# Prompt attention on one Trainium2 core: two heads side by side in four strips, scores ahead of transposes, and the selected keys made by GpSimd

## The reference

```python
def nsa_prompt(h, w_in, w_out, pe, w1, w2):
    q, z, kv, gl = nsa_project(h, w_in)          # 16 heads of 64, 4 key/value groups
    kc, c_end = compress(kv[:, :, 0], ...)       # 31 compressed keys, and values
    ks_blk, vs_blk = to_blocks(kv[:, :, 2]), to_blocks(kv[:, :, 3])
    kvw = kv[:, :, 4:6]                          # window branch
    ...
def nsa_core(...):
    # per branch: s = q k^T / 8 - slope * distance, masked softmax, p v
    o = g[..., 0, :] * o_c + g[..., 1, :] * o_s + g[..., 2, :] * o_w
    ...
    y = (o * jax.nn.silu(z)) @ w_out
```

## Time and profile before

| | |
|---|---|
| median of 3 runs | 1023.81 us (1022.68 to 1025.22) |
| the profiled execution | 1023.85 us |
| its span | 1022.0 us |
| busy over the span | PE 94%, DVE 63%, ACT 39%, POOL 38% |
| mean granted TensorE clock | 0.963 of full speed |

### The profile page before, as it was taken

How to read it: one execution, slowest core, us unless ns; L and a number is a source line. 1 busy time by engine, 2 the same in 40 slices (tenths; PEclk the granted TensorE clock), 3 DMA queues, 4 the chain that set the end, 5 groups by cost and what they waited for, 6 DMA issues and landing times.

```text
span 1022.0 us, 19230 instructions
## 1 busy us (share of the span) xinstructions
PE 964.4 (94%) x7148; PEld 816.7 (80%) x7148; DVE 648.7 (63%) x1398; ACT 403.5 (39%) x793; POOL 392.7 (38%) x330
## 2 busy tenths in 40 slices
PE   4999999999999969999799998999879999999995
PEld 3999989998899829999699868999757777764584
DVE  4799998899989779320662221153688888864403
ACT  5433443333333286221431101244557777751001
POOL 1698888788878779001020000000233333300000
PEclk9999999999999979999799998999879999999997
DMA  8334543454335360351158005221180000043002
GB/s 354 104 105 126 163 128 104 111 147 159 105 105 133 103 263 1 124 192 62 38 185 190 1 1 214 85 82 63 54 287 1 1 0 1 25 181 145 1 1 88
DMA packets 43016, 108.01 MB, mean 106 GB/s; under 512 B 20674, under 2 KB 21730, under 8 KB 38530
## 3 DMA queue, kind: packets, MB, share of 16 engines
q1 hardware_dynamic: 42658, 106.45, 32.0%
q10 hardware_dynamic: 288, 0.54, 0.1%
HBM read 81.87 MB, written 12.17 MB: 92 GB/s over the span
## 4 chain that ended last, share of the span: by engine, by line
PE 82%; DVE 7%; issue 4%; ACT 3%; POOL 3%; DMA 0%; DVEq 0%; ACTq 0%
PE ps L579 54%; PE ps L980 7%; PE ps L602 4%; PE ps L868 4%; POOL C L1781 3%; PE ps L756 3%; PE ps L856 2%; DVE SX L1565 1%; DVE KL L1534 1%; PE ps L548 1%; DVE C L1368 1%; PE ps L845 1%; PE ps L820 1%; PE ps L847 1%; PE ps L864 1%
## 5 line engine op out<-in xcount | busy, mean ns | idle before, releaser
L579 PE MATMUL ps<-Hh,ringAh 128*128 128x256 f32 (+1 forms) x768 | 161.2, 291 | 4.6 <-DVE Xl L1304 4.6
L1346 DVE SCALAR_TENSOR_TENSOR acc<-VP,tapc,acc 128x512 f32<-128x512 f32 x122 | 159.9, 1311 | 1.8 <-ACT acc L1092 1.7
L579 PE MATMUL ps<-Hh,ringAl 128*128 128x256 f32 (+1 forms) x768 | 159.4, 289 | 0.0
L579 PE MATMUL ps<-Xl,ringAh 128*128 128x256 f32 (+1 forms) x768 | 158.2, 287 | 0.0
L1744 POOL TENSOR_TENSOR ringAl<-ringA,ringAh 128x1024 fp32r<-128x1024 f32 x48 | 120.7, 2529 | 65.2 <-ACT ringAh L1058 58.0
L579 PEld LDWEIGHTS ps<-Hh,ringAh 128*128 128x128 f32 x768 | 123.3, 189 | 17.5 <-issue 17.5
L579 PEld LDWEIGHTS ps<-Xl,ringAh 128*128 128x128 f32 x768 | 124.1, 189 | 0.0
L579 PEld LDWEIGHTS ps<-Hh,ringAl 128*128 128x128 f32 x768 | 123.1, 189 | 0.0
L1346 DVE SCALAR_TENSOR_TENSOR ps<-VP,tapc,ps 128x512 f32<-128x512 f32 x138 | 102.9, 745 | 0.6
L868 PE MATMUL ps<-PTB,V 128*128 128x512 f32 (+3 forms) x256 | 91.0, 439 | 2.6 <-ACT PTB L1243 2.2
L579 PE MATMUL ps<-Hh,ringEh 128*128 128x256 f32 (+1 forms) x384 | 84.7, 303 | 7.1 <-DVE ringEl L1411 4.6
(11 more groups left out here) (239 smaller groups left out, 2017.6 us busy)
## 6 DMA issues: line engine op xcount, KB each, us to landing
ringA<-in_w_a SPq DMA_DIRECT2D x16, 1536.0 KB, 7.5
G<-VP SPq DMA_DIRECT2D x60, 260.0 KB, 4.8
ringE<-in_w_f SPq DMA_DIRECT2D x24, 512.0 KB, 3.5
ringC<-in_w_c SPq DMA_DIRECT2D x8, 1024.0 KB, 6.0
cache_cmp<-in_cache_cmp SPq DMA_DIRECT2D x32, 128.0 KB, 2.7
cache_sel<-in_cache_sel SPq DMA_DIRECT2D x16, 256.0 KB, 3.0
cache_win<-in_cache_win SPq DMA_DIRECT2D x1, 4096.0 KB, 13.6
out_win_s<-in_win_state SPq DMA_DIRECT2D x1, 4032.0 KB, 17.6
```

Of the source, the lines that this page charges most:

```text
L579: mm = nc.tensor.matmul(dst, w, x[:, cols], start=begins, stop=ends)
L1346: nc.vector.scalar_tensor_tensor(tap_sum(k % 2), src, w, tap_sum(k % 2), ALU.mult, ALU.add).then_inc(conv_step, 1)
```

## The change

- The units of a pair come in another order: `unit(u)` gives, in four groups of four units, for branch 0 then 1: query tiles 0 and 1 of both heads, then query tiles 2 and 3 of both heads.
- `pv` makes the values of both heads at once, in four strips of 32 columns: strips 0 and 1 take head 0's weights and the first group's values, strips 2 and 3 head 1's. It runs four times a pair, all of a group of units together, in one PSUM bank of 128 rows, which alternates between pairs. The compressed product is made once a pair. Weights lie in PTA (tiles 0 and 1) and PTB (2 and 3).
- A unit's scores are issued ahead of the transposes, which lag five units instead of four.
- `gate_heads` gates both heads with one instruction.
- Queries have two sets of buffers, so GpSimd makes those of a pair during the pair before. Its bias pieces follow after the last scores that read the old ones.
- GpSimd, not ScalarE and VectorE, makes KS[0] and the selected low keys, after the stored keys have landed (`k_stored`). VectorE makes the window low keys of group pair 0 only; GpSimd makes those of group pair 1 after its second step.
- TensorE's loop over pairs is written out; VectorE's and GpSimd's loops hold two pairs.

```diff
+def unit(u):
+    m = u // 4
+    return u % 4 // 2, m // 2, 2 * (m % 2) + u % 2
...
+        QS = [[at("QS00", [P, NP_], NR - 2048, F32R), at("QS01", [P, NP_], PTR + NP_ * 4, F32R)],
+              [at("QS10", [P, NP_], SMT + 2 * P * 4, F32R), at("QS11", [P, NP_], NR + 4 * (NKEY + P) * 4, F32R)]]
+        PTA = at("PTA", [P, 2, 2, 2, 2, P], HR)
+        PTB = at("PTB", [P, 2, 4, 2, P], HR + 8 * 2 * P * 4)
...
+                r, b, t = unit(u)
+                q = QS[i % 2][r][:, t * P:(t + 1) * P]
+                if u < 4 and u % 2 == 0:
                     pe.wait_ge(ql_set, 2 * i + r + 1)
+                if u == 0 and i == 0:
+                    pe.wait_ge(kl_ready, 4)
+                elif u == 8 and i == 0:
+                    pe.wait_ge(kl1_ready, 4)
+                elif u == 8 and i == 4:
+                    pe.wait_ge(kl1_last, 4)
+                if u >= 4 or i >= 1:
                     pe.wait_ge(sc_ready, 16 * i + u - 3)
+                nc.tensor.matmul(ps[:, u % 4, 0:n], q, KS[b][:, 2 * gp + r, 0:n], start=True, stop=False)
+                nc.tensor.matmul(ps[:, u % 4, 0:n], q, KL[r][:, b, gp, 0:n], start=False, stop=True).then_inc(qk_done, 1)
...
+            def pv(i, m):
+                gp, b, late = i // 4, m // 2, m % 2
+                bank = 6 + i % 2
+                if m == 0:
+                    if i == 0:
+                        pe.wait_ge(cs_kept, 4)
+                        pe.wait_ge(pt_zeroed, 1)
+                    if i >= 2:
+                        pe.wait_ge(og, i - 1)
+                    pe.wait_ge(pc_set, i + 1)
+                    nc.tensor.matmul(ps[:, bank], vcd[:, gp, :], PT[:, 0, :], start=True, stop=False)
+                pe.wait_ge(pt_kept, 16 * i + 4 * m + 4)
+                for k in range(2 + 2 * late):
+                    first = max(k, 2 * late)
+                    for j in range(4):
+                        v = b * GROUPS * HD + gp * P + 32 * j
+                        src = (PTB[:, j // 2, k] if late else PTA[:, b, j // 2, k])[:, first % 2:2, :]
+                        mm = nc.tensor.matmul(ps[32 * j:32 * j + 32, bank, P * first:P * (2 + 2 * late)], V[:, k, v:v + 32],
+                                              src.rearrange("p t q -> p (t q)"), start=False, stop=(b == late == 1 and k == 3))
+                mm.then_inc(pv_done, 1)
...
+                    qk(i, u, i // 4)
+                    if u >= 5:
+                        transpose(i, u - 5)
+                    elif i >= 1:
+                        transpose(i - 1, u + 11)
+                    if u % 4 == 2:
+                        if u >= 8:
+                            pv(i, u // 4 - 2)
+                        elif i >= 1:
+                            pv(i - 1, u // 4 + 2)
+            for u in range(11, 16):
+                transpose(7, u)
+            pv(7, 2)
+            pv(7, 3)
...
-                if t == 3:
-                    act.wait_ge(cs_step, 9 * 3 + 1)
-                    for r in range(2):
-                        for half in range(2):
-                            nc.scalar.activation(KS[0][HD * half:HD * half + HD, r::2, :],
-                                                 KTm[HD * r:HD * r + HD, 0, :, 0:NP_], ACT.Copy).then_inc(kh_ready, 1)
...
+                if u == 4 and reaches(i, 1):
+                    act.wait_ge(pv_done, 4 * i)
+                elif u == 12:
+                    act.wait_ge(pv_done, 4 * i + 2)
+                elif u % 8 == 0 and reaches(i, 1):
+                    act.wait_ge(pv_done, 4 * i - 3 + 2 * b)
+                dst = PTA[:, b, r, 0:t + 1, t % 2, :] if t < 2 else PTB[:, r, 0:t + 1, t % 2, :]
+                nc.scalar.activation(dst, ps[:, 4 + u % 2, 0:(t + 1) * P].rearrange("p (k q) -> p k q", q=P),
                                      ACT.Copy).then_inc(pt_kept, 1)
...
+            for r in (1, 0):
+                rows = slice(HD * r, HD * r + HD)
+                dve.wait_ge(kh1_ready, 4)
+                if r == 0:
+                    dve.wait_ge(kl1_ready, 2)
+                for half in (1, 0):
+                    nc.vector.tensor_tensor(KL[r][HD * half:HD * half + HD, 1, 0, 0:NP_], KTm[rows, 1, 0, 0:NP_],
+                                            KS[1][rows, r, :].bitcast(F32), ALU.subtract).then_inc(kl1_ready, 1)
...
+            def gate_heads(i, par):
+                dve.wait_ge(pv_done, 4 * i + 4)
+                nc.vector.tensor_tensor(ZT[:, i, 0:NP_], ps[:, 6 + par], ZT[:, i, 0:NP_], ALU.mult).then_inc(og, 1)
...
-                    if u == 5 and reaches(i, 1):
-                        gate_head(i - 1, 0)
-                    if u == 13 and reaches(i, 1):
-                        gate_head(i - 1, 1)
+                    if u == 8 and reaches(i, 1):
+                        gate_heads(i - 1, 1 - par)
...
+            pool.wait_ge(zeros_set, 1)
+            pool.wait_ge(k_stored, 16)
+            for i, (r, half) in enumerate(((0, 0), (0, 1), (1, 0), (1, 1))):
+                nc.gpsimd.tensor_copy(KS[0][HD * half:HD * half + HD, r::2, :],
+                                      KTm[HD * r:HD * r + HD, 0, :, 0:NP_]).then_inc(kh_ready, 1)
+                pool.wait_ge(kh_ready, i + 1)
+            for i, (r, half) in enumerate(((1, 1), (1, 0), (0, 1), (0, 0))):
+                rows = slice(HD * r, HD * r + HD)
+                nc.gpsimd.tensor_tensor(KL[r][HD * half:HD * half + HD, 0, :, 0:NP_], KTm[rows, 0, :, 0:NP_],
+                                        KS[0][rows, r::2, :].bitcast(F32), ALU.subtract).then_inc(kl_ready, 1)
+                pool.wait_ge(kl_ready, i + 1)
...
-            def head(i, r):
+            def query(i, par, r):
                 rows, other = slice(HD * r, HD * r + HD), slice(HD - HD * r, 2 * HD - HD * r)
-                if reaches(i, 1):
-                    pool.wait_ge(qk_done, 16 * i + 8 * r - 8)
+                q = QS[par][r]
+                if reaches(i, 2):
+                    pool.wait_ge(qk_done, 16 * i - 18 + 2 * r)
                 if r and not reaches(i, 1):
                     pool.wait_ge(f_done, FT)
-                if r or reaches(i, 1):
-                    pool.wait_ge(bias_set, 2 * i + r)
-                nc.gpsimd.tensor_copy(QS[r][rows, :], QT[rows, i, 0:NP_]).then_inc(qh_set, 1)
+                nc.gpsimd.tensor_copy(q[rows, :], QT[rows, i, 0:NP_]).then_inc(qh_set, 1)
                 pool.wait_ge(qh_set, 2 * i + r + 1)
                 nc.gpsimd.tensor_tensor(ptick[other, r:r + 1], ones[other, 0:1], ones[other, 0:1], ALU.mult)
-                nc.gpsimd.tensor_tensor(QS[r][other, :], QT[rows, i, 0:NP_], QS[r][rows, :].bitcast(F32),
+                nc.gpsimd.tensor_tensor(q[other, :], QT[rows, i, 0:NP_], q[rows, :].bitcast(F32),
                                         ALU.subtract).then_inc(ql_set, 1)
+                pool.wait_ge(ql_set, 2 * i + r + 1)
+            def distance(i, r):
                 if reaches(i, 1):
-                    pool.wait_ge(sc_ready, 16 * i + 8 * r - 8)
+                    pool.wait_ge(sc_ready, 16 * i - 2 + 2 * r)
                 elif r == 0:
                     pool.wait_ge(f_done, FT - 1)
-                pool.wait_ge(ql_set, 2 * i + r + 1)
                 nc.gpsimd.tensor_tensor(bias[:, r, :], dist[:], slopes[:, i, r:r + 1].to_broadcast([P, NP_]),
                                         ALU.mult).then_inc(bias_set, 1)
+                pool.wait_ge(bias_set, 2 * i + r + 1)
             def compressed(i):
                 if reaches(i, 1):
-                    pool.wait_ge(pv_done, 4 * i - 1)
+                    pool.wait_ge(pv_done, 4 * i - 3)
                 else:
                     pool.wait_ge(cs_kept, 4)
-                pool.wait_ge(bias_set, 2 * i + 2)
-                if not reaches(i, 1):
                     nc.gpsimd.memset(PT[HD:P, 0, :], 0.0).then_inc(pt_zeroed, 1)
                     pool.wait_ge(pt_zeroed, 1)
                 nc.gpsimd.tensor_copy(PT[0:HD, 0, :], PCT[:, i, :]).then_inc(pc_set, 1)
+                pool.wait_ge(pc_set, i + 1)
+            def step(i, par):
+                query(i, par, 0)
+                if not reaches(i, 1):
+                    distance(i, 0)
+                query(i, par, 1)
+                if not reaches(i, 1):
+                    distance(i, 1)
                 compressed(i)
+                if reaches(i, 1):
+                    distance(i, 0)
+                    distance(i, 1)
+            def last_low_keys():
+                pool.wait_ge(kh1_ready, 4)
+                for i, (r, half) in enumerate(((1, 1), (1, 0), (0, 1), (0, 0))):
+                    rows = slice(HD * r, HD * r + HD)
+                    nc.gpsimd.tensor_tensor(KL[r][HD * half:HD * half + HD, 1, 1, 0:NP_], KTm[rows, 1, 1, 0:NP_],
+                                            KS[1][rows, 2 + r, :].bitcast(F32), ALU.subtract).then_inc(kl1_last, 1)
+                    pool.wait_ge(kl1_last, i + 1)
+            step(0, 0)
+            step(1, 1)
+            last_low_keys()
```

(3 more changed lines are left out.)

125 lines of the change are left out of this document (25 added, 100 removed).

## The result

The changed kernel takes 1005.86 us (median of 4 runs, 1003.69 to 1007.2) against 1023.87: ratio 0.9822, 95% interval 0.98 to 0.9843. That is 18 us faster; 34 were forecast. The time lies 0.14 us inside the upper end of the range (976 to 1006), which is less than its own runs differ: that it lies inside is luck.

A forecast was written before the change was run, and what follows sets the result against it. TensorE bounded steady pairs before; after, VectorE at 17.3 us plus 0.2 was to set a 17.5 us period. 24.2 (pairs) + 11.5 (start) + 0.5 - 1.0 - 1.0 = 34.2 us gained, 1023.85 to 989.6 us, range 976 to 1006.

The forecast's parts named there:

- Rivals 5 and 6: Steady pairs: TensorE's clock falls to 1.2 GHz, 1097 us, chance 3%; value-product strips don't overlap, 1074 us, chance 2%.
- rival 3: Steady pair: GpSimd's burst is exposed whole on VectorE, period 20.4 us, total 1010 us, chance 6%.
- The coupling term: Steady pair: next scores stand behind value-product bursts, against TensorE's lead over VectorE; 0.2 us a pair added.
- rival 2: Steady pair: TensorE's bursts meet a VectorE without buffer, or small units wait for exp; period 18.8, 999 us, chance 16%.
- the 1.5 us a pair of before: Steady pair: VectorE's normalizations lengthened beside GpSimd's query work, 2 x 0.72 us, taken as the same after the change.
- The start: From the projections' end to pair 1: GpSimd makes keys early, TensorE reaches pair 1 11.5 us sooner, bounds 7 and 14.
- rival 4: Start: first scores wait for something else (last projection's gate, exp's table load), gain 0 there, 1001 us, chance 5%.
- the cover: Start: TensorE windows left at 1.2 GHz were to be hidden under VectorE's work; no cost added.
- (a): Ahead of the attention: GpSimd's casts run beside VectorE's two low weights, TensorE waits; 0 to 2.4 us, 1.0 taken.
- (b): Pair 1: GpSimd's four low window key pieces of the second group pair beside VectorE; 0 to 5.1 us, 1.0 taken.
- (c): Drain after the last pair: 7.2 us in place of 7.7, gain 0.5.
- (d): Loads that follow (weights, cached keys): their counts come as early as before against their use, 0.

## Why the prediction was right in its direction and short in its size

**TensorE.** Right: the four strips start within 0.02 us of each other (832.13 to 832.15; 32 take 1.65 us), the compressed product is made once a pair, the pair costs TensorE 16.9 us against 16.4, and it no longer bounds by its work alone. Rivals 5 and 6 (clock, strips) are out, and so is rival 3: one normalization a steady pair takes over 1 us. Strips cost 4 x 0.22 = 0.9 us a pair, where 0.8 was taken. The 0.17 us of drain that the prediction cites stands in the Trainium skill (TensorE: Matmul & The Clock Gate) under Single matmul latency, not under Step-by-step; its estimate of 1.4 us was too high.

**The coupling term: this step failed.** "1.7 + 0.54 for the next score pair against a lead of 2 to 2.5 us is close; I add 0.2." Measured, VectorE is idle 1.8 us a pair, not 0.2. The lead in units is what the order says, not what is there when the burst begins: in the place shown it was 1.5 us against the 2 to 2.5 of the prediction, and 2.4 - 1.5 = 0.9 us of idle time followed. TensorE has itself waited 0.7 us, four times a pair, for weights that VectorE and ScalarE pass on late, and VectorE had stood behind the burst before. That each wait hands the next one on is read from the rows, not tried; that bursts and order set VectorE's waits two runs show: spreading the products took 0.9 us of idle time away, and putting transposes first added 1.0. It is the mechanism of rival 2, priced at 18.8 there (chance 16%). It makes 1.6 us x 7 = 11 us of the 15.4 that are missing in pairs and drain.

**GpSimd beside VectorE: mis-sized.** The prediction kept the 1.5 us a pair of before, since "after each piece VectorE has a score to read, which isn't held up". That scores aren't held is right (384 columns take 0.55 us 9 times beside a GpSimd tensor_tensor and 0.55 us 23 times away from one), but a normalization or the copy stands next to each piece. That the bias pieces ran "beside work now at no visible price" was misread: in the kernel before, from 779 to 905, the 512-column normalization on SX, which meets them, takes 0.1 us more than on S, 0.2 us a pair.

```profile
L1565 DVE TENSOR_SCALAR SX<-SX,gsc,gpair 128x512 f32<-128x512 f32 x12 | 7.8, 646 | 0.0
...
L1565 DVE TENSOR_SCALAR S<-S,gsc,gpair 128x512 f32<-128x512 f32 x12 | 6.5, 543 | 0.0
```

With bias and query cut 2.65 us of busy time went, so VectorE's pair is 17.85, not 17.3: 0.55 x 7 = 4 us. The copy of the gates, which is the same as before but now stands in GpSimd's burst, has no place in the prediction: it takes 1.27 us, and leaving it out gave 5.8 us. The exclusive lock that the Trainium skill tells of (SBUF — State Buffer, shared port pair) fits these rows; its worst case (20.4 us) did not come: 2.65 us a pair are held, where every piece exposed whole would be 4.6.

**The start: 7.0 us, not 11.5**, from the end of the projections to pair 1 (27.3 before, 20.3 after); its lower bound was 7. Scores at 733.9 and keys from 627 to 644 came as forecast; undoing the keys costs 5.4. What was missed: the table load (rival 4 names it, the sum leaves it out) and last copy on ScalarE, behind which VectorE is idle 1.71 us, and the cover: "some windows at 1.2 GHz will stay, under VectorE's cover". The first burst fell into one, and VectorE was idle meanwhile (3.62 us ahead of 749.55).

**Small terms.** (a) The two low weights take VectorE 3.65 us beside GpSimd's casts, against 2.35; the first, for which TensorE waits, takes 1.61 us of the chain of waits in place of 1.15, so 0.45 where 1.0 was taken. (b) The last low keys in pair 1: 1.0 taken; some 2, by the run that moves them, with the clock's share of the 2.8 taken off. (c) Pair 7 and drain gained 2.5, of which a pair's gain is 1.4, so 1.1 against 0.5. (d) Nothing, as said.

Together: pairs and drain gave 9.3 us where 24.2 + 0.5 stood, the start 7.0 where 11.5 stood, and 1.9 of the 18.3 lie ahead of the attention, 1.6 of them ahead of all that the change touches, so they are not its work.

Open: what sets the granted clock in the first pair (0.83, 0.91 and 1.00 in three kernels that differ little there), and how the strips' own share stands beside the order's and the keys', since strips were not undone alone; nor was the new order of the units.

## What to carry to other kernels

When engines hand work round in a ring and are well filled (here VectorE 91%, TensorE 86%, ScalarE 76% of a steady pair), the busiest one's time is a lower bound and not the period: add what each waits, from bursts counted in microseconds against the buffers between the engines, and spread a burst that is longer than that lead. Spread only the long ones, since every switch into strips costs. A burst that moves must be held against every instruction of the other engine that now stands beside it, however small it is.

## What was not expected of the hardware

- A VectorE copy of 128x16 takes 0.175 us in the kernel before and 1.27 beside a GpSimd tensor_tensor. Scores, which read PSUM and their bias in SBUF, are not stretched (0.55 us for 384 columns beside one and away from one).
- Going into 32-column strips and back costs 0.22 us a group (1.65 against 1.43 us for the same columns, and 0.78 against 0.57 for a burst with half the instructions).
- The granted clock was 1.00 in the first 8 us of the attention, in which TensorE was busy 4.4 us, then 0.61 from 742 to 746 and 0.54 from 746 to 750, where TensorE was busy again (3.29 and 4.00 of 4 us).
